# Where one product's copy is kept, and the order of copies, folds and first pair, in three Winograd feed-forwards

## The reference

```python
def swiglu(h, w_gate, w_up, w_down):
    return (jax.nn.silu(h @ w_gate) * (h @ w_up)) @ w_down
x = x + MACARON_WEIGHT * swiglu(rmsnorm_2(x, norm_g[i, k]), ffn_w_gate, ffn_w_up, ffn_w_down)
```

## Time and profile before

| | us |
|---|---|
| runs before (3) | 2790.58, 2791.79 (median), 2792.29 |
| profiled execution, its own time | 2789.91 |
| its span, first to last instruction | 2788.1 |
| TensorE busy in the span | 2700.4 (97%) |
| VectorE, ScalarE, GpSimd busy | 1714.3, 1285.7, 1239.8 |
| mean granted TensorE clock | 0.995 |

### The profile page before, as it was taken

How to read it: one execution, slowest core, us unless ns; L and a number is a source line. 1 busy time by engine, 2 the same in 40 slices (tenths; PEclk the granted TensorE clock), 3 DMA queues, 4 the chain that set the end, 5 groups by cost and what they waited for, 6 DMA issues and landing times.

```text
span 2788.1 us, 42307 instructions
## 1 busy us (share of the span) xinstructions
PE 2700.4 (97%) x14754; PEld 2247.6 (81%) x14754; DVE 1714.3 (61%) x2598; ACT 1285.7 (46%) x2179; POOL 1239.8 (44%) x607
## 2 busy tenths in 40 slices
PE   9999999999999999999999999989999999999998
PEld 7777777888888888858879888889989754889897
DVE  5886533755534224167888667795857565868484
ACT  4455433444333223253246444564535666655353
POOL 3334433444454444514126565546646411456563
PEclk9999999999999999999999999999999999999999
DMA  4333322323332323313113232322322210233222
GB/s 167 120 98 122 99 76 62 99 97 98 106 105 92 97 97 99 113 53 105 35 61 122 90 121 71 110 90 93 124 73 91 90 32 17 90 121 106 91 91 76
DMA packets 88520, 257.84 MB, mean 92 GB/s; under 512 B 11576, under 2 KB 16696, under 8 KB 88138
## 3 DMA queue, kind: packets, MB, share of 16 engines
q1 hardware_dynamic: 81872, 244.74, 26.6%
q10 hardware_dynamic: 6522, 11.43, 1.2%
HBM read 249.98 MB, written 6.03 MB: 92 GB/s over the span
## 4 chain that ended last, share of the span: by engine, by line
PE 65%; issue 16%; DVE 8%; POOL 7%; ACT 3%; ACTq 0%; POOLq 0%; DVEq 0%; DMA 0%
PE ps L935 13%; PE ps L936 13%; PE ps L937 13%; POOL wlo L884 4%; POOL wlo L866 3%; PE ps L1456 3%; PE ps L1458 3%; PE ps L1457 3%; DVE ps L2624 2%; DVE ps L2547 1%; PE ps L1673 1%; PE ps L1655 1%; PE ps L1642 1%; PE ps L1325 1%; PE ps L1354 1%
## 5 line engine op out<-in xcount | busy, mean ns | idle before, releaser
L866 POOL TENSOR_TENSOR wlo<-raw,whi 128x1024 fp32r<-128x1024 f32 x317 | 780.6, 2468 | 1130.4 <-ACT whi L1752 1106.1
L1456 PE MATMUL ps<-fold,whi 128*128 128x256 f32 x1848 | 530.9, 287 | 55.5 <-ACT scratch L1963 41.5
L1457 PE MATMUL ps<-fold,whi 128*128 128x256 f32 x1848 | 523.9, 284 | 0.0
L1458 PE MATMUL ps<-fold,wlo 128*128 128x256 f32 x1848 | 523.9, 284 | 0.0
L1752 ACT ACTIVATE whi<-raw 128x1024 fp32r<-128x1024 f32 x320 | 333.8, 1052 | 336.0 <-PE ps L937 159.9
L935 PE MATMUL ps<-lin_hi,whi 128*128 128x512 f32 x1144 | 452.0, 395 | 0.0
L937 PE MATMUL ps<-lin_hi,wlo 128*128 128x512 f32 x1144 | 445.4, 389 | 0.0
L936 PE MATMUL ps<-lin_lo,whi 128*128 128x512 f32 x1144 | 445.3, 389 | 0.0
L1456 PEld LDWEIGHTS ps<-fold,whi 128*128 128x128 f32 x1848 | 355.4, 192 | 69.9 <-ACT scratch L1963 51.6
L1457 PEld LDWEIGHTS ps<-fold,whi 128*128 128x128 f32 x1848 | 355.8, 193 | 0.9 <-issue 0.5
L1458 PEld LDWEIGHTS ps<-fold,wlo 128*128 128x128 f32 x1848 | 355.6, 192 | 0.0
(11 more groups left out here) (479 smaller groups left out, 5028.7 us busy)
## 6 DMA issues: line engine op xcount, KB each, us to landing
raw<-in_packs SPq DMA_DIRECT2D x324, 512.0 KB, 3.5
raw_pair_even<-in_packs SPq DMA_DIRECT2D x66, 512.0 KB, 4.2
raw_pair_odd<-in_packs SPq DMA_DIRECT2D x66, 512.0 KB, 4.3
table<-bias_scratch ACTq DMA_DIRECT2D x12, 256.0 KB, 3.3
bias_scratch<-biasrow ACTq DMA_DIRECT2D x16, 160.0 KB
x<-in_x_t SPq DMA_DIRECT2D x4, 512.0 KB, 7.6
out_t<-x SPq DMA_DIRECT2D x14, 128.0 KB, 1.8
bias_scratch<-biasrow ACTq DMA_DIRECT2D x4, 320.0 KB
```

Of the source, the lines that this page charges most:

```text
L866: pool.tensor_tensor(wlo[:, n % 4, :], raw[:, n % 2, :], whi[:, n % 4, :].bitcast(F32), ALU.subtract).then_inc(low_split, 1)
L1456: pe.matmul(target, wh, folds[c][:, fold, 0, :], start=begins and c == 0, stop=False, skip_group_check=True)
L1457: pe.matmul(target, wh, folds[c][:, fold, 1, :], start=False, stop=False, skip_group_check=True)
L1458: mm = pe.matmul(target, wl, folds[c][:, fold, 0, :], start=False, stop=c == 3, skip_group_check=True)
```

## The change

The copy of M5 goes to the free half of M5's own PSUM bank instead of SBUF, and quarter 3 reads it there. On ScalarE `hidden_split` of the pair before goes behind the copies of M5 and U2, on VectorE `low_hidden` goes behind quarter 0. In the folds T1 is split with side 0 (five splits a pair of chunks where there were four), and T2 and T4 come ahead of T3. The third step of `first_pair` on ScalarE moves from ahead of the last fold to behind it. In the first pair `stats` goes behind product 4 instead of 3, and `root` behind the copy of U3.

```diff
@@ -61,7 +61,7 @@
 GROUPS, FIRST_TILE, DOWN_PACK, GROUP_AT = (6, 8, 8), (16, 0, 8), (2, 0, 1), (0, 6, 14)
 SEVENS = ("ffn1", "ffn2", "ffn3")
 FOLDS = (5, 6, 8)
-CHUNK_BASE = [8 * _s + 8 * sum(_f < _s for _f in FOLDS) for _s in range(10)]
+CHUNK_BASE = [8 * _s + 12 * sum(_f < _s for _f in FOLDS) for _s in range(10)]
 
 SLOTS, PACK_BASE, PAIRED, PAIR_BASE = 0, {}, {}, {}
 _paired = _pairs = 0
@@ -1449,7 +1449,7 @@
                 slot, half, bank, fold, begins = PRODUCTS[k]
                 for c in steps:
                     if s is not None:
-                        pe.wait_ge(chunk_ready, CHUNK_BASE[s] + 4 * c + (1, 2, 2, 3, 3, 4, 4)[fold])
+                        pe.wait_ge(chunk_ready, CHUNK_BASE[s] + 5 * c + (1, 3, 3, 2, 5, 4, 4)[fold])
                     at = half * T + c * P
                     wh, wl = whi[:, slot, at:at + P], wlo[:, slot, at:at + P]
                     target = ps[:, banks[bank], 0:T // 2]
@@ -1484,7 +1484,7 @@
                 if k in (2, 4, 6):
                     pe.wait_ge(terms_copied, value(i, 8, 4 * pair + (1, 3, 4)[k // 2 - 1]))
                 product(k, (3,) if early else range(4)).then_inc(packs_used if k in BY_WEIGHT else product_made, 1)
-                if k == 3 and s is not None:
+                if k == 4 and s is not None:
                     stats(s, FOLD_STAT)
             if outs is not None:
                 pe.wait_ge(outs_done, outs + 8)
@@ -1838,22 +1838,22 @@
 
         def fold(s, j):
 
-            c, side, n = j // 2, j % 2, 8 * (s - 1) + j
-            d = BY_PAIRS[j]
-            at = COLS_OF_SET[s] + d
-            act.wait_ge(chunk_ready, CHUNK_BASE[s] + 4 * c)
+            c, side, d = j // 2, j % 2, BY_PAIRS[j]
+            made, at = 12 * FOLDS.index(s) + 3 * c, COLS_OF_SET[s] + d
+            act.wait_ge(chunk_ready, CHUNK_BASE[s] + 5 * c)
             act.activation(gained[:, side, :], x[:, d, :], ACT.Copy, scale=cols[:, at:at + 1]).then_inc(gain_applied, 1)
-            act.wait_ge(gain_applied, n + 1)
+            act.wait_ge(gain_applied, 8 * (s - 1) + j + 1)
             if side == 0:
                 act.activation(folds[c][:, 0, 0, :], gained[:, 0, FIRST_HALF], ACT.Copy).then_inc(chunk_high, 1)
-                square(s, j)
-                return
-            act.activation(folds[c][:, 1:3, 0, :], gained[:, 1, :].rearrange("p (u t) -> p u t", u=2), ACT.Copy).then_inc(chunk_high, 1)
+                act.wait_ge(fold_made, made + 1)
+                act.activation(folds[c][:, 3, 0, :], gated[:, FIRST_HALF], ACT.Copy).then_inc(chunk_high, 1)
+            else:
+                act.activation(folds[c][:, 1:3, 0, :], gained[:, 1, :].rearrange("p (u t) -> p u t", u=2), ACT.Copy).then_inc(chunk_high, 1)
+                act.wait_ge(fold_made, made + 2)
+                act.activation(folds[c][:, 5:7, 0, :], upped[:, :].rearrange("p (u t) -> p u t", u=2), ACT.Copy).then_inc(chunk_high, 1)
+                act.wait_ge(fold_made, made + 3)
+                act.activation(folds[c][:, 4, 0, :], gated[:, LAST_HALF], ACT.Copy).then_inc(chunk_high, 1)
             square(s, j)
-            for k, source in enumerate((gated, upped)):
-                act.wait_ge(fold_made, 8 * FOLDS.index(s) + 2 * c + k + 1)
-                act.activation(folds[c][:, 3 + 2 * k:5 + 2 * k, 0, :], source[:, :].rearrange("p (u t) -> p u t", u=2),
-                               ACT.Copy).then_inc(chunk_high, 1)
 
         def residual_to_pairs(phase, s, name):
 
@@ -1861,10 +1861,11 @@
             for j in range(DC):
                 if j < DC - AHEAD:
                     split_high(base + j)
-                else:
+                elif j < DC - 1:
                     first_pair(name, 0, j - (DC - AHEAD))
                 act.wait_ge(outs_done, OUT_BASE[phase] + j + 1)
                 fold(s, j)
+            first_pair(name, 0, 2)
 
         def last_residual(phase, s):
 
@@ -1960,7 +1961,8 @@
             else:
                 act.wait_ge(product_made, value(i, 6, 3 * pair + k))
             bank = 3 * (p % 2) + (0, 2, 0, 0)[k]
-            act.activation(terms[p % 2][:, k, :], ps[:, bank, FIRST_HALF], ACT.Copy).then_inc(terms_copied, 1)
+            target = ps[:, bank, LAST_HALF] if k == 1 else terms[p % 2][:, k, :]
+            act.activation(target, ps[:, bank, FIRST_HALF], ACT.Copy).then_inc(terms_copied, 1)
 
         def silu(name, g, p, i, n):
             act.wait_ge(quarter_steps, value(i, 10, 5 * (PAIR_BASE[f"{name}_up{g}"] + p) + 3))
@@ -1986,21 +1988,18 @@
             if next_packs is not None:
                 act.wait_ge(product_made, 3 * (PAIR_BASE[f"{name}_up{g}"] + p) + 1)
             ahead(0)
-            if p:
-                hidden_split(name, g, p - 1, i, n)
             copy_term(name, g, p, i, 1)
             if next_packs is None:
                 split_sum(name, g, p + 1, 0, i)
             copy_term(name, g, p, i, 2)
+            if p:
+                hidden_split(name, g, p - 1, i, n)
             if next_packs is None:
                 split_sum(name, g, p + 1, 1, i)
+            ahead(1)
+            copy_term(name, g, p, i, 3)
             if s is not None:
                 root(s, FOLD_STAT)
-                copy_term(name, g, p, i, 3)
-                ahead(1)
-            else:
-                ahead(1)
-                copy_term(name, g, p, i, 3)
             ahead(2)
 
         def seven_up(name, g, n, s):
@@ -2027,11 +2026,13 @@
                 for j in range(DC):
                     if j < DC - AHEAD:
                         split_high(down + AHEAD + j)
-                    else:
+                    elif g < 2 or j < DC - 1:
                         first_pair(name if g < 2 else after, (g + 1) % 3, j - (DC - AHEAD))
                     if g == 2:
                         act.wait_ge(outs_done, OUT_BASE[f"{name}_down2"] + j + 1)
                         fold(s + 1, j)
+                if g == 2:
+                    first_pair(after, 0, 2)
 
 
         act.dma_start(cols[:, 0:N_COLS], A["cols"]).then_inc(cols_arrived, 16)
@@ -2566,9 +2567,9 @@
 
         def fold_low_part(s, c, k):
 
-            dve.wait_ge(chunk_high, CHUNK_BASE[s] + 4 * c + k + 1)
-            where = (slice(0, 1), slice(1, 3), slice(3, 5), slice(5, 7))[k]
-            source = (gained[:, 0, FIRST_HALF], gained[:, 1, :], gated[:, :], upped[:, :])[k]
+            dve.wait_ge(chunk_high, CHUNK_BASE[s] + 5 * c + k + 1)
+            where = (slice(0, 1), slice(3, 4), slice(1, 3), slice(5, 7), slice(4, 5))[k]
+            source = (gained[:, 0, FIRST_HALF], gated[:, FIRST_HALF], gained[:, 1, :], upped[:, :], gated[:, LAST_HALF])[k]
             dve.tensor_tensor(folds[c][:, where, 1, :], source.rearrange("p (u t) -> p u t", t=T // 2),
                               folds[c][:, where, 0, :].bitcast(F32), ALU.subtract).then_inc(chunk_ready, 1)
 
@@ -2577,14 +2578,16 @@
             c, side = j // 2, j % 2
             dve.wait_ge(gain_applied, 8 * (s - 1) + j + 1)
             b11, b12, b21, b22 = [gained[:, r, half] for r in range(2) for half in (FIRST_HALF, LAST_HALF)]
+            t1, t2, t3, t4 = gated[:, FIRST_HALF], upped[:, FIRST_HALF], gated[:, LAST_HALF], upped[:, LAST_HALF]
             if side == 0:
-                order(dve.tensor_tensor(gated[:, FIRST_HALF], b12, b11, ALU.subtract))
+                dve.tensor_tensor(t1, b12, b11, ALU.subtract).then_inc(fold_made, 1)
                 fold_low_part(s, c, 0)
+                fold_low_part(s, c, 1)
             else:
-                dve.tensor_tensor(gated[:, LAST_HALF], b22, b12, ALU.subtract).then_inc(fold_made, 1)
-                order(dve.tensor_tensor(upped[:, FIRST_HALF], b22, gated[:, FIRST_HALF], ALU.subtract))
-                dve.tensor_tensor(upped[:, LAST_HALF], b21, upped[:, FIRST_HALF], ALU.subtract).then_inc(fold_made, 1)
-                for k in range(1, 4):
+                order(dve.tensor_tensor(t2, b22, t1, ALU.subtract))
+                dve.tensor_tensor(t4, b21, t2, ALU.subtract).then_inc(fold_made, 1)
+                dve.tensor_tensor(t3, b22, b12, ALU.subtract).then_inc(fold_made, 1)
+                for k in range(2, 5):
                     fold_low_part(s, c, k)
             dve.wait_ge(squares_ready, 8 * s + j + 1)
             dve.wait_ge(squares_summed, 8 * s + j)
@@ -2606,7 +2609,8 @@
 
             pair, n, b = PAIR_BASE[f"{name}_up{g}"] + p, PACK_BASE[f"{name}_up{g}"] + 4 * p, 3 * (p % 2)
             both, gates = ps[:, b, :], ps[:, b + 1, :]
-            m1, m5, u2, u3 = [terms[p % 2][:, t, :] for t in range(4)]
+            m1, u2, u3 = [terms[p % 2][:, t, :] for t in (0, 2, 3)]
+            m5 = ps[:, b + 2, LAST_HALF]
             if k == 0:
                 dve.wait_ge(packs_used, value(i, 8, n + 2))
                 dve.wait_ge(terms_copied, value(i, 8, 4 * pair + 1))
@@ -2621,7 +2625,7 @@
             elif k == 3:
                 dve.wait_ge(packs_used, value(i, 8, n + 4))
                 dve.wait_ge(terms_copied, value(i, 8, 4 * pair + 4))
```

(6 more changed lines are left out.)

## The result

| | before | after |
|---|---|---|
| median of the runs, us | 2791.78 (4 runs, 2790.58 to 2792.29) | 2750.14 (4 runs, 2749.83 to 2751.49) |
| profiled execution, its own time, us | 2789.91 | 2750.08 |
| its span, us | 2788.1 | 2748.3 |

The ratio after to before is 0.9852, with a 95% interval of 0.9835 to 0.9869. The forecast was 2750.0, the range 2741 to 2766.

A forecast was written before the change was run, and what follows sets the result against it. TensorE, busy 2700.4 of 2788.1 us, was taken as the bound, its idle or slow time winnable. Gains 42.4 + 1.3 less 2.0 give 41.7 us: 2789.9 to 2748.2, with the median 1.9 higher 2750 us; range 2741 to 2766.

The forecast's parts named there:

- M5's copy in its bank: Middle pair: ScalarE's copy of M5 into PSUM takes 0.38 us; quarter 3 then takes 0.43 us instead of 2.31.
- half of the waits would stay: Rival, chance 0.08: M5's copy into PSUM takes about 2.3 us, product 4 waits near 0.5 us, time 2771 us.
- What GpSimd's hold does next: Middle pair: `pair_sum` 0 inherits part of the wait, ends near 2.8 us, `make_hidden` 3.4; VectorE about 8.6 a pair.
- ScalarE's order: Middle pair: U2 is copied by 4.8 us, product 4 may start at 5.8; its wait goes, 1.0 us to spare.
- term 42.4 us: Middle pairs of the three feed-forwards: the 42 waits of 1.00 to 1.06 us ahead of product 4 all go.
- Folds: Ahead of the first pairs: about +0.7 us per even chunk, up to +1.6 us at the last `take`, ffn3 +1.1.
- First pair: ffn2's product 2 starts at 1831.9 instead of 1830.1, after M1's copy; ffn1 about +1.3 us, ffn3 +1.2.
- What comes back: Up to second pair's product 2: `root` starts once stats are there; net +1.0 us ffn1, +0.9 ffn2, +0.1 ffn3.
- The clock in the first pair: First pairs: slow stretch of ffn1 and ffn2 unchanged; half a slow stretch counted for ffn3, within its 0.1 us.
- signs of being right: Line 1963's waits fall to about 6, quarter 3 near 0.43 us, middle pair 10.1, first pairs wait for M1's copy.
- signs of being wrong: Middle waits left before product 4, VectorE over 10 us a pair, new weight low-part wait, first pairs changed over 4 us.
- The sum: Whole kernel: 42.4 + 1.3 - 2.0 = 41.7 us gained; 2748.2 profiled, median 1.9 above that before, forecast 2750.

The follow-up runs named there:

- the orders alone: Kernel before with only `hidden_split` moved behind M5's and U2's copies on ScalarE and the hidden low part behind quarter 0 on VectorE: 2744.24 us.
- run with filled waits: Changed kernel with 28, 20 and 10 idle matmuls in the waits ahead of product 2 of the three first pairs: 2746.64 us.

## Why the prediction was right, and where it wasn't

*M5's copy in its bank.* Right: 0.37 us for the taken 0.38, quarter 3 at 0.43 us. That half of the waits would stay fell with it.

*What GpSimd's hold does next.* Right: the sum ended at 1510.19, 2.9 us after the last matmul of the pair before (1507.61 - 0.28), for 2.8 in the text; `make_hidden` (1510.10, 0.68 us) 3.5 us after, for 3.4. VectorE is busy 8.85 us a pair for the 8.6 of the text.

*ScalarE's order.* Right in its result. But the two parts were costed as if both were needed; each alone takes the 42 waits away. The term 42.4 us was 1.9 us short: it counted the waits, while a pair lost 1.055 us, a little more than its wait of 1.01. VectorE's load didn't need the cure either: with the orders alone it was busy 10.03 us a pair.

*Folds.* Right in direction: the last take came 2.4 us later in ffn2's first pair (4.60 us after the first product for 2.18), where the text had 1.6. That term was 0.8 us short. In ffn1 and ffn3 product 2 came 1.1 and 0.9 us later, for 1.3 and 1.2 in the text.

*First pair.* The wait only changed its place, as predicted: M1's copy in ffn2 came at 1818.39, 5.3 us after the last take at 1813.11 (5.6 predicted). The step that failed is "What comes back", that `root` starts as soon as stats are there, together with the clock (below). Of the 1.8 us lost up to product 2, ffn2 should have won 0.9 back by the second pair's. Product 2 came 2.4 us later (10.31 us after the first product for 7.88), and from there to product 2 of the second pair another 1.0 us was lost (14.85 for 13.81). In ffn1 0.1 us came back for 0.3, in ffn3 0.8 for 1.1. The run with `stats` and `root` undone shows one reason: their new place costs 2.8 us in the whole kernel, 0.9 of it in this stretch of ffn2, where the clock is down, against 0.2 and 0.3 in ffn1 and ffn3. The run with filled waits shows the other: with `root` in its new place but the clock up, the stretch took 13.05 us, so that 0.8 did come back.

*The clock in the first pair.* "I take the slow stretch of ffn1 and ffn2 as unchanged" failed too. The stretch of ffn2 lasted until 1825, about 6 us from 1818.82 on and twice as long as the 3 us before, and a second one of 1.5 us, which the text didn't have, came in the second pair. The half stretch that was counted for ffn3 did not come.

*The signs.* Of the signs of being right most came: 6 waits (9.5 us, for 7 to 9), quarter 3 at 0.43, a pair of 10.1 us, a longer `pair_sum` 0, the wait ahead of product 2. But two of the signs of being wrong came as well, both in the first pairs: a new wait for line 884 (2.6 us), and 4.7 us lost there where more than 4 was the mark.

*The sum.* The first pairs and what follows cost 6.2 us (4.7 and 1.5) where 2.0 were taken; the middle pairs and the second pairs' waits gave 45.7 where 43.7 were taken. So the profiled execution came at 2750.08 and not at 2748.2. The forecast of 2750 adds 1.9 us because the median before stood above its profiled execution; after, the median is 0.06 us from it. Two errors of about 2 us cancel, and the hit within 0.2 us is luck at that size.

What stays open: why the same wait of 2.2 us was followed by a slow stretch in ffn2 and not in ffn3 (in all traces together such waits, 2.24 to 2.26 us ahead of product 2 of a second pair, were followed by one in five cases of seven), and whether the folds' own price can be had without the slow clock; the latter wasn't tried alone.

## What to carry to other kernels

When a wait is cut by two edits at once, ask what each leaves alone: here either the freed operand or the order of the copies gave the whole 45 us, and the third part of the change, aimed at waits of 10 us, moved them to the next copy and cost 5 to 7. Moving a step "behind" another on an engine's list also puts it behind that step's own wait: U3's copy, now ahead of `root`, waited 1.89 us for TensorE. Idle time of TensorE is to be priced with the slow clock that may follow it, but only where TensorE is the next thing late: filling it gave 3.5 us in one place and nothing clear of the noise in the other.

## What the runs showed of the hardware

- A copy of 256 columns by ScalarE from PSUM takes 0.37 us into PSUM and 0.38 into SBUF.
- A VectorE sum of two SBUF operands ended 0.55 us after the GpSimd split that was running when it came, and got in ahead of the next split, even when those stood back to back: 1.50, 1.75 and 2.87 us for the same kind of sum, against 0.69 us without one. The next 512-column split then took 1.75 us instead of 1.29.
- TensorE's granted clock was 1.00 after an idle time of 2.94 us (ffn3) and 0.72 to 0.71 after 3.39 us; in ffn2 it fell to 0.50 after one of 2.24 us, both 9 us after an earlier slow stretch (the changed kernel) and with none before it (the waits filled); in ffn3 a wait of 2.25 us left it at 1.00.
- With the orders alone, VectorE was busy 10.03 of 10.10 us in a middle pair and TensorE had no wait there.
